# A trunk of one decoder layer on one core: every buffer behind the normalised input moved by 64 bytes

## The reference

```python
h = rmsnorm(x, norm_mix)
proj = h @ w_in                       # 1024 x 5656: q, k, v of two attentions, gates
y_a = nsa_attention(...)              # 8 heads: compressed, selected and window attention
y_b = dilated attention               # 12 heads in 3 groups, merged by their denominators
merged = sigmoid(g_A) * (y_a @ w_up_nsa) + sigmoid(g_B) * (y_b @ w_up_dil)
x = x + merged @ w_out
h = rmsnorm(x, norm_ffn)
gt, up = split(h @ w_ffn_in)          # 1024 x 5632
x = x + (silu(gt) * up) @ w_ffn_out   # 2816 x 1024
out = rmsnorm(x, norm_final)
```

## The kernel before

| Region | Operands | Before | After |
|---|---|---|---|
| A | n_hi, n_lo (also the merged sum), a_hi, a_lo, t_lo | 0 | 0 |
| E | y_hi, y_lo | 0 | 64 |
| B | w_hi, w_lo (all units, and the weight sums) | 0 | 64 |
| C | t_hi | 0 | 64 |
| Dd | h_hi, h_lo, wa_hi of slot 0 | 0 | 64 |
| G | wa22_hi, wa22_lo of both slots | 0 | 64 |
| H | wa_lo of slot 0, wa_hi and wa_lo of slot 1 | 64 | 0 |

## Time and profile before

### The profile page before, as it was taken

One profiled execution on the slowest core, in us unless ns is written; L12 is line 12 of the kernel. 1 busy time (PEld: TensorE's weight loads), 2 busy tenths in 40 slices (PEclk: granted clock), 3 DMA queues, 4 the chain that ended last, 5 costly groups with the idle time before them and its releaser, 6 DMA issues.

```text
span 783.5 us, 12585 instructions
## 1 busy us (share of the span) xinstructions
PE 775.8 (99%) x4994; PEld 676.3 (86%) x4994; DVE 485.5 (62%) x920; ACT 327.2 (42%) x597; POOL 154.6 (20%) x111
## 2 busy tenths in 40 slices
PE   9999999999999999999999999999999999999996
PEld 7878899889878787788888988999999999888885
DVE  5935432555776767656625668898788876332347
ACT  5212055254446666653313624444444443222145
POOL 1300100000000000002200185876666650000000
PEclk9999999999999999999999999999999999999999
DMA  6941336250311111036331731334333335333302
GB/s 217 339 154 54 108 61 155 57 167 4 109 54 55 55 55 41 23 98 190 108 108 54 229 94 55 108 109 117 104 104 107 108 109 192 130 108 107 107 1 107
DMA packets 101286, 83.50 MB, mean 107 GB/s; under 512 B 16960, under 2 KB 94832, under 8 KB 101232
## 3 DMA queue, kind: packets, MB, share of 16 engines
q1 hardware_dynamic: 100992, 82.46, 35.2%
q10 hardware_dynamic: 240, 0.29, 0.1%
HBM read 77.44 MB, written 5.29 MB: 106 GB/s over the span
## 4 chain that ended last, share of the span: by engine, by line
PE 99%; DMA 0%; ACT 0%; DVE 0%; issue 0%; ACTq 0%; DVEq 0%
PE bank L1681 28%; PE bank L1682 28%; PE bank L1683 28%; PE bank L1914 2%; PE bank L1933 2%; PE bank L1901 2%; PE bank L1815 1%; PE bank L1856 1%; PE bank L1837 1%; PE bank L1778 1%; PE bank L1722 1%; PE bank L1705 1%; PE bank L1728 1%; PE bank L1928 1%; PE bank L1731 0%; PE bank L1868 0%
## 5 line engine op out<-in xcount | busy, mean ns | idle before, releaser
L1028 DVE TENSOR_TENSOR w_lo<-w_raw,w_hi 128x2048 fp32r<-128x2048 f32 (+2 forms) x29 | 64.5, 2224 | 79.5 <-ACT w_hi L677 79.4
L1681 PE MATMUL bank<-n_hi,w_hi 128*128 128x512 f32 x272 | 108.8, 400 | 0.0
L1683 PE MATMUL bank<-n_hi,w_lo 128*128 128x512 f32 x272 | 106.1, 390 | 0.0
L1682 PE MATMUL bank<-n_lo,w_hi 128*128 128x512 f32 x272 | 106.0, 390 | 0.0
L677 ACT CAST w_hi<-w_raw 128x2048 fp32r<-128x2048 f32 (+2 forms) x29 | 53.6, 1848 | 61.8 <-PE bank L1683 51.1
L1681 PE MATMUL bank<-w_hi,a_hi 128*128 128x512 f32 (+1 forms) x180 | 69.3, 385 | 0.0
L633 POOL TENSOR_TENSOR n_lo<-merge_tmp,n_hi 128x512 fp32r<-128x512 f32 x8 | 10.4, 1298 | 298.2 <-ACT n_hi L859 298.2
L1682 PE MATMUL bank<-w_lo,a_hi 128*128 128x512 f32 (+1 forms) x180 | 69.2, 384 | 0.0
L1683 PE MATMUL bank<-w_hi,a_lo 128*128 128x512 f32 (+1 forms) x180 | 69.2, 384 | 0.0
L1681 PE MATMUL bank<-w_hi,n_hi 128*128 128x256 f32 (+2 forms) x192 | 62.1, 323 | 0.0
L1683 PE MATMUL bank<-w_hi,n_lo 128*128 128x256 f32 (+2 forms) x192 | 61.4, 320 | 0.0
(11 more groups left out here) (268 smaller groups left out, 1927.4 us busy)
## 6 DMA issues: line engine op xcount, KB each, us to landing
w_raw<-in_w_ffn_in_dram SPq DMA_DIRECT2D x44, 512.0 KB, 5.0
w_raw<-in_w_in_dram SPq DMA_DIRECT2D x37, 512.0 KB, 4.9
w_raw<-in_w_ffn_out_dram SPq DMA_DIRECT2D x22, 512.0 KB, 4.2
w_raw<-in_w_out_dram SPq DMA_DIRECT2D x8, 512.0 KB, 4.1
w_raw<-in_w_in_dram SPq DMA_DIRECT2D x12, 256.0 KB, 4.7
xs<-in_x_dram SPq DMA_DIRECT2D x4, 512.0 KB, 4.6
wck_k<-in_w_ck_dram SPq DMA_DIRECT2D x1, 2048.0 KB, 11.8
wck_v<-in_w_cv_dram SPq DMA_DIRECT2D x1, 2048.0 KB, 15.0
```

The source lines that it names most:

```text
L1028: dve.tensor_tensor(wlo[u % 2][:, 0:n], raw[u % 2][:, 0:n], whi[u % 2][:, 0:n].bitcast(F32), ALU.subtract).then_inc(lo_done, 1)
L1681: pe.matmul(dst, w[0], x_[0], start=start, stop=False)
L1682: pe.matmul(dst, w[0], x_[1], start=False, stop=False)
L1683: return pe.matmul(dst, w[1], x_[0], start=False, stop=stop)
```

## The change

The start of region E, and with it that of every region behind it, moves up by 64 bytes. Three buffers are placed anew so that all still fits: `nsa_bias0` and the `wa_lo` of slot 1 sit 128 bytes lower within H, and `rhalf`, which lay between, moves to the end of G. `tanh_g`, which nothing used, is dropped. Every engine has the same instructions in the same order as before; only addresses differ, and the lines from L311 on carry numbers lower by one.

```diff
         A = BASE
-        E = A + 32768
+        E = A + 32768 + 64
         Fo = E + 26624
...
-        nbias = [at("nsa_bias0", [2, S], H + 14464), at("nsa_bias1", [2, S], E + 16384)]
+        nbias = [at("nsa_bias0", [2, S], H + 14336), at("nsa_bias1", [2, S], E + 16384)]
...
-        rhalf = at("rhalf", [2, TT], H + 14368)
+        rhalf = at("rhalf", [2, TT], G + 17536)
...
-        tg = at("tanh_g", [2, S], A + 61440)
...
-                for j, o, o2 in ((0, H + 8192, G + 6656), (1, H + 14464, G + 10752))]
+                for j, o, o2 in ((0, H + 8192, G + 6656), (1, H + 14336, G + 10752))]
```

## The result

The changed kernel takes 788.38 us in the median of four runs (787.24 to 789.62), the kernel before 784.19 in the same comparison (784.10 to 785.71): a ratio of 1.0054 with a 95% interval of 1.0042 to 1.0066. It is slower by some 4 us; 770.0 was predicted. The profiled execution of the change took 787.7 us, with a span of 785.9. The time ahead of the projections differs from execution to execution (the projections begin at 20.7 to 22.7 us in the nine profiles of the whole layer, at 22.45 in that of before and at 21.55 in that of the change), so what the change costs is read from the lengths of the stretches.

What follows compares the result with a forecast made beforehand. TensorE was taken as the bound, so only shorter matmuls save time: 10.5 us (512-wide) plus 3.9 (256-wide) is 14.4, less 0.3 is 14.1, giving 769.4 from the 783.5 span, plus 0.6: 770.0 us; range 766 to 781.

Steps and rivals of the forecast that it cites:

- What bounds the kernel: Whole kernel: TensorE busy 775.8 of 783.5 us, so time comes out only if a matmul itself gets shorter.
- The predicted pairs and their counts: Operand pairs with n, a or t_lo going from 0 to 64 apart: 1572 matmuls of 512 columns, 584 of 256.
- the price of the 512-wide: Matmuls with 512 columns and n or a as an operand: each 6.7 ns shorter, 1572 x 6.7 = 10.5 us gained.
- The first, only the 256-wide gain: Rival: 512-wide matmuls already run undisturbed and gain nothing, only 256-wide ones gain 3.9 us; 780.2 us, chance 0.15.
- Slower: Rival: each 512-wide matmul pays 6.7 ns more, +10.5 - 3.9 = +6.6 us; 790.7 us, chance 0.07.
- The 256-wide: Matmuls of 256 columns with n stationary, t_lo moving or a stationary: 584 x 6.7 ns = 3.9 us gained.
- Modulo 128: All affected operand pairs: addresses 64 apart modulo 128 save 6.7 of 13.3 ns a matmul, whatever the region.
- The Trainium skill's rule of two ports: TensorE reads moving and stationary operands through independent ports, so addresses cannot matter; 784.1 us, within the no-change rival, chance 0.07.
- The scale of the cost: Skill's N / 2.4 + 2.5 ns against traced paces: at most 11 ns a matmul, 24 us in all (760).
- The sum: Whole kernel: 10.5 + 3.9 = 14.4 us, less 0.3 for compression matmuls and some tile ends, so 14.1 us gained.

## Why the prediction was wrong

- **What bounds the kernel: right.** TensorE stays the bound; no wait was added, and PE's waits after are those of the start. The predicted pairs and their counts are right too: only those stretches changed in which n, a or t_lo meets a weight, and the 280-wide took 128.6 ns before and after. One pair was overlooked: wa_lo of slot 1, set 128 bytes lower, goes from a distance of 64 to 192 from h; its pace stayed at 113.3.
- **The step that failed** is the price of the 512-wide: "I take 6.7 ns, since the 13.3 ns is the same for 256 and 512 at residue 0, as if paid once per weight load and not per column", so 1572 x 6.7 = 10.5 us gained. Measured: n moving pays 6.6 ns more (816 in the projections; from start to start that form took 190.4 us there before and 194.85 after, +4.45, less than 816 x 6.6: behind a break for attention's small matmuls the aligned pairs of before too were slow at first, 231.7 ns for the second and 226.6 for the eleventh in the mean of 33 breaks), n stationary 2.2 more (192, +0.4), a stationary 2.2 more (516, +1.1). An offset of 64 never brings 512 columns under 226.7; a multiple of 256 is the best distance found for them. Nor was the same extra at both widths a reading: once the difference between the two widths, 106.7, is taken as the price of every 256 columns, what remains is the same 13.3 at both, whatever its cause. At distance 0 the 512-wide had nothing to give that any distance tried here would take; the 256-wide had 6.7 ns.
- **The rivals.** The first, only the 256-wide gain, was right that the 512-wide had nothing to gain (226.7 is 2 x 113.3, the best pace found at either width), and wrong that an offset costs them nothing. "Slower" described it, +6.7 for each 512-wide, but named one price for all; its 790.7 against 788.4 comes mostly from the 708 matmuls with n or a stationary that pay a third of it. That 788.4 lies so near is in part luck: the 256-wide gained 2.6 us instead of 3.9, which made up for some of that. I gave it 0.07 against 0.62 for the forecast, though neither had a row behind it: the trace held no 512-wide pair that was off. The 280-wide rows, the only ones with a longer pass, showed no gain, and I set them aside. They could not have shown the price either: the two steps compared there are at distances 64 and 128 modulo 256, which at 512 columns cost the same 233.3.
- **The 256-wide.** 584 x 6.7 = 3.9 us was taken from h on wa. t met its sum: the stretch of seven products is 2.0 us shorter (1.8 predicted), though of each three only the matmul with t_lo has another distance and the gain is spread over all three, at 117.8 each (the mean of 120.0 twice and 113.3). n stationary gave 120.0 - 117.8 = 2.2 ns, 288 x 2.2 = 0.6 us instead of 1.9: it is at -64, and stays at the slower of the two paces.
- **Modulo 128.** "I read it as the residue and not the region" was right, but the modulus was not 128. With 256 and a sign, the rows of slot 1 hold distances of 192 and 64 and could not have told these from one another.
- **The Trainium skill's rule of two ports** ("TensorE: Matmul & The Clock Gate", section "Step-by-step: what each phase is for"), from which the prediction took that addresses cannot matter, does not agree with these runs: streams at 226.7 and 233.3 ns differ in nothing but addresses.
- **The scale of the cost.** The Trainium skill ("TensorE: Matmul & The Clock Gate", section "Back-to-back issue gap") gives the formula behind 760 us for a matmul by itself, not for pairs of weight load and matmul as here; no stream of these runs settled under 226.7 ns at 512 columns or 113.3 at 256.
- **The sum.** +3.8 in the projections (4.45 less 0.6), +0.4, +1.1, -2.0: 3.3 us, against -14.1 predicted. The 0.6 us between span and median is no cost of launch: on record every execution takes 1.7 to 1.9 us more than its span, so the profile of before is of an execution of some 785.3 us. The forecast, 14.1 off the median, does not depend on it.

## What to carry to other kernels

A price read from matmuls of one width is no price for another width: where the trace holds no matmul of the shape in question, the sign is as open as the size, and the likeliest single value is no forecast. Where operands are placed by hand, look at the stationary address minus the moving one modulo 256: here, with a new stationary operand for each matmul, 0 was best for 512 columns of float32r, and 64 to either side for 256 columns, so an offset belongs to the units of one width and not to a region that both widths share. And where TensorE gets faster in a stage, look at the engine behind it: VectorE, 139 of 170 us busy before, was at 161 of 172 in one of these layouts.

## What the hardware showed that I had not expected

- The pace of a matmul with a new stationary operand each time depends on the distance of its two operands modulo 256, with its sign: at 512 columns 226.7 ns at 0, 233.3 at +64 and 128, 229 at -64 (save one stream of four, at 233.3); at 256 columns 120.0 at 0. When n went to the other side of the weights, 233.3 and 229 changed places.
- At 256 columns and a distance of +64 or -64 the same two addresses run at 113.3 or 117.8 ns, by what ran before.
- The offset that helps 256 columns by 2 to 7 ns costs 512 columns 2 to 7 ns.
- At 512 columns and distance 0 the best pace comes only after some ten matmuls: behind a break 231.7 ns for the second, 226.6 for the eleventh. At +64 it is 233 to 234 from the second on.
- VectorE's subtraction of 128 x 1024 took 1262 ns or 2216 ns in the mean, in two layouts that differ in addresses alone; in the slow one GpSimd's sums ran beside it and took 2.2 us instead of 1.3. That TensorE's changed pace had moved them there is likely and not shown.
